# Attention in a two-block language-model kernel: where the next head's Q and K are projected

## What is computed

```python
proj = rmsnorm(x, norm1_g) @ w_in          # dq, dk, dv, fq, fk, fv are slices of it
# diff, for each block of 128 queries:
sc = einsum('bqhcd,bkhcd->bchqk', qb, k) * scale + bias     # causal, -inf above the diagonal
p = softmax(sc);  w = p[:, 0] - lam * p[:, 1];  out = einsum('bhqk,bkhd->bqhd', w, v)
y_diff = rmsnorm(out, diff_subln_g) * (1 - lam_init)
# fox:
sc = einsum('bqhd,bkhd->bhqk', qb, k) * scale + decay       # decay from a running sum, causal
out = einsum('bhqk,bkhd->bqhd', softmax(sc), v)
```

## Time and profile before

| | us |
|---|---|
| median of 3 runs | 3777.13 (3776.09 to 3777.54) |
| the profiled execution | 3780.0 |
| its span (first to last instruction) | 3777.9 |
| TensorE busy in the span | 3231.9 (86%) |
| the two attention stages, from the first V matmul of one to the last `YL` of the other | 87.6 to 717.6 |

### The profile page before, as it was taken

How to read it: one execution, slowest core, us unless ns; L and a number is a source line. 1 busy time by engine, 2 the same in 40 slices (tenths; PEclk the granted TensorE clock), 3 DMA queues, 4 the chain that set the end, 5 groups by cost and what they waited for, 6 DMA issues and landing times. The chain is left out here.

```text
span 3777.9 us, 42591 instructions
## 1 busy us (share of the span) xinstructions
PE 3231.9 (86%) x15247; PEld 2628.9 (70%) x15247; DVE 1374.8 (36%) x2195; ACT 1122.4 (30%) x1533; POOL 771.7 (20%) x510
## 2 busy tenths in 40 slices
PE   5999999899998999899999993586888788996686
PEld 3777777688776777688788872475677676885465
DVE  3244133211155122434434334742224443214743
ACT  3334243212266121412222223122233331332221
POOL 0100100022111121212122110431222221223621
PEclk6999999999999999899999996777899998998878
DMA  2110101022211222311111102403110000211102
GB/s 105 28 34 17 45 23 42 18 67 58 64 38 37 67 68 84 68 39 58 42 47 53 33 28 67 64 0 98 37 39 23 22 22 23 50 50 51 56 17 112
DMA packets 270465, 178.76 MB, mean 47 GB/s; under 512 B 65960, under 2 KB 246312, under 8 KB 269872
## 3 DMA queue, kind: packets, MB, share of 16 engines
q1 hardware_dynamic: 270384, 177.69, 16.8%
HBM read 158.43 MB, written 19.23 MB: 47 GB/s over the span
## 5 line engine op out<-in xcount | busy, mean ns | idle before, releaser
L136 POOL TENSOR_TENSOR w_low<-w_raw,w_high 128x1024 fp32r<-128x1024 f32 (+1 forms) x183 | 418.0, 2284 | 2009.3 <-ACT w_high L129 2004.4
L154 PE MATMUL pu<-act_high,w_high 128*128 128x512 f32 x1104 | 432.8, 392 | 9.5 <-POOLq L108 8.3
L154 PE MATMUL pu<-act_low,w_high 128*128 128x512 f32 x1104 | 431.9, 391 | 0.0
L154 PE MATMUL pu<-act_high,w_low 128*128 128x512 f32 x1104 | 431.7, 391 | 0.0
L129 ACT ACTIVATE w_high<-w_raw 128x1024 fp32r<-128x1024 f32 (+1 forms) x183 | 182.7, 999 | 442.8 <-PE po L950 94.3
L154 PE MATMUL pg<-act_high,w_high 128*128 128x512 f32 x576 | 228.0, 396 | 55.6 <-POOL w_low L136 29.6
L154 PEld LDWEIGHTS pu<-act_high,w_high 128*128 128x128 f32 x1104 | 208.9, 189 | 54.4 <-POOLq L108 9.1
L154 PEld LDWEIGHTS pu<-act_high,w_low 128*128 128x128 f32 x1104 | 208.7, 189 | 43.5
L154 PEld LDWEIGHTS pu<-act_low,w_high 128*128 128x128 f32 x1104 | 208.8, 189 | 43.3
L154 PE MATMUL pg<-act_low,w_high 128*128 128x512 f32 x576 | 226.8, 394 | 0.0
L154 PE MATMUL pg<-act_high,w_low 128*128 128x512 f32 x576 | 226.5, 393 | 0.0
(11 more groups left out here) (508 smaller groups left out, 6788.8 us busy)
## 6 DMA issues: line engine op xcount, KB each, us to landing
w_raw<-in_w_in SPq DMA_DIRECT2D x110, 512.0 KB, 4.2
w_raw<-in_ffn_up SPq DMA_DIRECT2D x44, 512.0 KB, 3.9
w_raw<-in_w_out SPq DMA_DIRECT2D x24, 512.0 KB, 3.9
v_raw<-in_ffn_down SPq DMA_DIRECT2D x11, 1024.0 KB, 5.1
acum_rows<-acum_rows SPq DMA_DIRECT2D x16, 512.0 KB, 3.8
x<-in_x SPq DMA_DIRECT2D x8, 512.0 KB, 8.5
bias<-neg_c SPq DMA_DIRECT2D x4, 1024.0 KB, 5.1
m_part<-gate SPq DMA_DIRECT2D x8, 512.0 KB, 3.1
```

The source lines that it names most:

```text
L136: pool.tensor_tensor(self.low[slot][:, 0:nk, :], self.raw[slot][:, 0:nk, :], self.high[slot][:, 0:nk, :].bitcast(F32), ALU.subtract).then_ ...
L154: last = pe.matmul(out[:, h, :] if not halves else out[h], w[slot][:, k, :], x[:, k, cols], start=(n == 0), stop=(n == 3 * nk - 1))
```

## The change

Q and K each get two buffers, so that the next head's can be written while this head's are read. One of the three transpose banks becomes `pP`, into which the next head's Q and K are projected, half by half (24 matmuls a half, four halves). The 96 matmuls are laid out by a table in 17 places of the head: 6 ahead of the first transposes, 4 to 6 ahead of each `values` and each `turned`, and 9 behind the last `values`. The copies out of `pP` stand at four places of ScalarE's list, the last behind its last transposed group. The loops are over pairs of heads, SyncE's is written out, and the weights of head h + 2 are asked for during head h. The first head's Q and K are projected ahead of the loop.

```diff
+NEXT_HEAD = (("first", 6), (("values", 0), 5), (("turned", 1), 5), (("values", 1), 4), (("turned", 2), 4),
...
+             (("values", 6), 5), (("turned", 7), 5), (("values", 7), 5), ("out", 9))
...
-        Q = sbuf(core, ctx, "q", [P, SEQ])
-        K = sbuf(core, ctx, "k", [P, SEQ])
+        Q = [sbuf(core, ctx, f"q{s}", [P, SEQ]) for s in range(2)]
+        K = [sbuf(core, ctx, f"k{s}", [P, SEQ]) for s in range(2)]
...
-        pT = [psum(core, ctx, f"pt{c}", [P, 4, P]) for c in range(3)]
+        pT = [psum(core, ctx, f"pt{c}", [P, 4, P]) for c in range(2)]
         pO = psum(core, ctx, "po", [P, 4, P])
+        pP = psum(core, ctx, "pp", [P, HALF])
...
-                def head(h, more):
-                    pe.wait_ge(sem("reduced"), h * U + 1)
-                    project(1, h + 2, pS[1])
+                def head(h, s, more):
+
+                    def ahead_of(t, count):
+
+                        for t in range(t, t + count):
+                            g, n = t // (3 * KD), t % (3 * KD)
+                            slot, half = g // 2, g % 2
+                            k, i = n // 3, n % 3
+                            if n == 0:
+                                if half == 0:
+                                    W.wait(pe, slot, h + 3)
+                                if g:
+                                    pe.wait_ge(sem("qk"), h * 4 + 4 + g)
...
-                            pe.wait_ge(sem("ev_act"), h * acts[GN] + acts[max(n - 2, 0)] + 1)
-                            pe.wait_ge(sem("ev_dve"), h * dves[GN] + dves[max(n - 2, 0)] + 1)
+                            pe.wait_ge(sem("ev_act"), h * acts[GN] + acts[max(n - 1, 0)] + 1)
+                            pe.wait_ge(sem("ev_dve"), h * dves[GN] + dves[max(n - 1, 0)] + 1)
...
                     scores(0)
                     scores(1)
+                    project_next("first")
                     turned(0)
                     for i in range(NB):
                         if i + 2 < NB:
                             scores(i + 2)
+                        project_next(("values", i))
                         values(i)
                         if i + 1 < NB:
+                            project_next(("turned", i + 1))
                             turned(i + 1)
-                    if more:
-                        pe.wait_ge(sem("reduced"), h * U + U + 1)
-                        project(0, h + 3, pS[0])
+                    project_next("out")
                     pe.wait_ge(sem("o_scaled"), h + 1)
...
+                        if more and i in TAKEN:
+                            take_next(TAKEN.index(i))
                         if i + 1 < NB:
                             evacuate(h, i + 1)
...
+                    if more:
+                        take_next(3)
 
                     if diff:
                         act.wait_ge(sem("mean"), h + 1)
```

More of the change, by code:

```diff
@@ L846, in _, with next_head_places @@
                 dve.tensor_tensor_scan(c[:, :], f[:, :], z[:, :], 0.0, ALU.mult, ALU.add).then_inc(sem("c"), 1)
+NEXT_HEAD = (("first", 6), (("values", 0), 5), (("turned", 1), 5), (("values", 1), 4), (("turned", 2), 4),
+             (("values", 2), 6), (("turned", 3), 6), (("values", 3), 6), (("turned", 4), 6),
+             (("values", 4), 6), (("turned", 5), 6), (("values", 5), 6), (("turned", 6), 6),
+             (("values", 6), 5), (("turned", 7), 5), (("values", 7), 5), ("out", 9))
+def next_head_places():
+    at, places, taken = 0, {}, []
+    for place, count in NEXT_HEAD:
+        places[place] = (at, count)
+        at += count
+        if at % (3 * KD) == 0 and place != "out":
+            taken.append(place[1] - 1)
+    assert at == 4 * 3 * KD and len(taken) == 3
+    return places, taken
 def stage_attention(core, kind, q_at, k_at, v_at, y0, ahead):
@@ L864, in stage_attention @@
     ends = {(i, c): n + 1 for n, (i, c, _, _) in enumerate(groups)}
+    PLACES, TAKEN = next_head_places()
     with stage(core) as (ctx, sem):
@@ L964, in project, with project_next @@
                                 n += 1
-                        last.then_inc(sem(f"half{slot}") if half == 0 else W.s("used", slot), 1)
-                def head(h, more):
-                    pe.wait_ge(sem("reduced"), h * U + 1)
-                    project(1, h + 2, pS[1])
+                        last.then_inc(sem("half") if half == 0 else W.s("used", slot), 1)
+                def head(h, s, more):
[9 more added lines that the diff above has]
+                                    pe.wait_ge(sem("qk"), h * 4 + 4 + g)
+                            w, x = ((W.high, AH), (W.high, AL), (W.low, AH))[i]
+                            last = pe.matmul(pP[:, :], w[slot][:, k, :], x[:, k, half * HALF:(half + 1) * HALF],
+                                             start=(n == 0), stop=(n == 3 * KD - 1))
+                            if n == 3 * KD - 1:
+                                last.then_inc(sem("half") if half == 0 else W.s("used", slot), 1)
+                    def project_next(place):
+                        if more:
+                            ahead_of(*PLACES[place])
                     def scores(i):
@@ L981, in scores @@
                                 rows = slice(64 * c, 64 * (c + 1))
-                                last[c] = pe.matmul(pS[c][:, a // HALF, 0:e - a], Q[rows, b * P:(b + 1) * P], K[rows, a:e],
+                                last[c] = pe.matmul(pS[c][:, a // HALF, 0:e - a], Q[s][rows, b * P:(b + 1) * P], K[s][rows, a:e],
                                                     start=True, stop=diff or e < n)
@@ L1041, in _ @@
                     pe.wait_ge(sem("mask16"), 2)
-                over_loop(pe, NH, head)
+                over_loop(pe, NH // 2, lambda pair, more: [head(pair * 2 + s, s, more or s == 0) for s in range(2)])
             @block.scalar
@@ L1101, in evacuate @@
                             act.wait_ge(sem("o"), h * U + 2 * (i - 1) + c + 1)
-                        act.activation(PT[:, c, g * P:(g + count) * P], flat(pT[n % 3])[:, 0:count * P], ACT.Copy).then_inc(sem("ev_act"), 1)
+                        act.activation(PT[:, c, g * P:(g + count) * P], flat(pT[n % 2])[:, 0:count * P], ACT.Copy).then_inc(sem("ev_act"), 1)
                 if diff:
                     act.wait_ge(sem("gain_scaled"), 1)
-                over_loop(act, NH, head)
+                over_loop(act, NH // 2, lambda pair, more: [head(pair * 2 + s, s, more or s == 0, more) for s in range(2)])
             @block.vector
```

77 lines of the change are left out of this document (50 added, 27 removed).

## The result

The changed kernel takes **3789.21 us** (median of nine runs, 3783.72 to 3794.78) where the kernel before takes 3777.54 (nine runs beside them): a ratio of 1.0025, with a 95% interval of 1.0015 to 1.0036. That is slower by about 12 us by the medians and 9 by the ratio (6 to 14 by its interval). The sign was forecast, and the time lies in the range of 3782 to 3812, but the size was forecast at +22, about twice as much. The profiled execution takes 3789.49 us with a span of 3787.6, against 3780.0 and 3777.9.

A forecast was written before the change was run, and what follows sets the result against it. TensorE was taken to bound the kernel, except for 4.8 us a head and the lower clock. Three diff heads (15.0), three fox heads (4.2) and two last heads (2.8) sum to +22 us: 3799 us, range 3782 to 3812.

The forecast's parts named there:

- The diff boundary: Between diff heads: 3.8 us idle ahead of the output transposes, 1.6 more ahead of second scores, together +5.4 us.
- The fox boundary: Between fox heads: the bias table's landing makes TensorE wait 2.6 us for second scores instead of 0.74, +1.9 us.
- The fill: Projections put into TensorE's gaps inside the blocks win 2.4 us a diff head, 2.2 a fox head.
- The banks: Two transpose banks make long blocks' transposes wait: net +1.3 us a diff head, +1.0 fox, 1.4 a last head.
- the clock: The low-clock dip moves from the blocks to the boundary and costs about the same 1.5 us a head.
- changes of matmul kind: At the 17 places switching from projection to other matmuls: 0.7 us a head, bounds 0 and 1.5.
- Rival (a): Boundary gaps don't lower the clock: 1.5 us back in six heads, 9 in all, 3790 us; chance 0.17.
- The rest of the program: No term for time outside the two attention stages; counted at nothing.

The follow-up runs named there:

- fox-only run: The change in the fox stage only, the diff stage running the code of the kernel before: 3775.94 us, 0.9988 against the kernel before.
- root first: The changed kernel with ScalarE's table load and square root ahead of the copy of K's second half in diff: 3776.76 us, 0.9995 against the kernel before.
- useless matmuls at the diff boundary: The changed kernel with 14 unread matmuls behind the last values of the three diff heads with a successor: 3789.19 us, 1.0027 against the kernel before.
- the last version: Changed kernel, table load and root before K's copy, 14 projections behind values, `YL` between reductions, bias asked early, projections between first scores and inside transposes: 3742.78 us.
- the early bias: The changed kernel with the bias table asked for right behind the head's last reduction: 3791.82 us, measured in one execution only.

## Why the prediction was right or wrong

**What held.** The diff boundary, in every step up to the output transposes: the copy of K ahead of the table load, the load uncovered, TensorE idle for 3.80 us (forecast 3.8). The table load takes 1.28 and the root starts 0.01 behind it (220.63, then 221.92), so the drain of 1.38 us that the Trainium skill ("ScalarE: Activation LUTs", What ACT_TABLE_LOAD costs) adds does not show ahead of the root; the prediction had counted none. The fox boundary: the bias landing sets the reduction (5.13 us from its issue to VectorE's start, forecast 5.2), TensorE waits 2.43 (forecast 2.6). The fill: the third scores' wait down to 0.77 (forecast 0.7), the waits for values gone. The banks: 0.30 to 0.62 in the four long blocks, forecast 0.45 to 0.76.

**How much the clock took.** The trace tells in which stretches TensorE was granted the lower of its two levels, 1.2 instead of 2.4 GHz. Work there takes twice as long (eight output transposes 1.97 us instead of 1.03), so half of TensorE's busy time in these stretches is an estimate of what the clock cost. One of them, in the first fox head of the kernel before (windows view, columns as above):

```profile
478.90:485.60 6.70, 6.36 (x30) 4.93 (x28) 2.78 (x11) 3.20 (x9) 0.00 (x0) 0.50 0.00 0
```

For the two fox heads of the fox-only run that do the same work, the estimate gives 1.46 us, and their busy times differ by 1.41. From the first V matmul of a stage to the next stage's (in fox to the last output transposes), in us:

| | length | TensorE idle | clock | other busy time |
|---|---|---|---|---|
| diff, before | 315.2 | 26.8 | 10.0 | 278.4 |
| diff, after | 330.3 | 36.9 | 14.2 | 279.2 |
| difference | +15.1 | +10.1 | +4.2 | +0.8 |
| forecast | +16.4 | +14.3 | 0 | +2.1 |
| fox, before | 312.0 | 21.7 | 11.9 | 278.5 |
| fox, after | 308.0 | 23.4 | 3.7 | 281.0 |
| difference | -4.0 | +1.7 | -8.2 | +2.5 |
| forecast | +5.6 | +3.5 | 0 | +2.1 |

(The forecast's idle column is its fill, banks and boundary terms with the last head, its other busy time the 0.7 a head for changes of matmul kind.)

**The step that failed: the clock.** "I expect the dip to move from the blocks to the boundary and to cost about the same 1.5 us." In fox it did not move: the three heads with a successor lost the dip in their blocks, no boundary of the profiled execution got one, and 8.2 us came back that the sum had at nothing. That is most of the 9.6 by which the fox stage missed. It is more than 1.5 a head, since in the kernel before the dips of the first and the last fox head lasted twice as long as the one that the prediction had priced from the earlier trace rows. The prediction argued from the earlier trace rows, a diff row with 3.13 us idle and output transposes behind it, for both stages; the fox boundary has no wait for `o_scaled`, and no row showed what its single gap of 2.6 us does to the clock.

In diff the dip did move to the boundary, and cost more: at the second boundary 0.94 in the output transposes (1.97 - 1.03), 0.31 in the first scores and 1.80 in the second ones (3.79 - 1.99). By the last diff head the low clock lasted through the boundary and into the blocks (0.85 for the whole window). That the diff stage all the same came out near its forecast, +15.1 for 16.4, is luck: the clock took 4.2 us that were not in the sum, the waits came out 4.2 below it and the other busy time 1.3 (the second scores waited 1.49, 1.43 and 1.43 where 2.35 was forecast, in part because the slow work ahead of them filled the time).

Rival (a), that the fill keeps the clock up, split by stage. It had 9 us back, half of them in diff; 8.2 came back in the fox stage and none in diff, so that its time, 3790, fits the result is in part luck too.

That filling the gap ahead of the third scores takes the dip from the blocks was shown from both sides: useless matmuls there made the kernel before 16 us faster, and taking the six projections out of it cost 17, some 13 of them by the estimate above as work at the half clock and most of the rest as waiting.

**Smaller misses.** A fox head adds up as boundary +1.7, fill -2.3, bank waits +0.85 (1.85 in four, against 1.0), clock -1.6, other busy time +0.65, together -0.7, and measures -0.9. So the 0.7 a head for changes of matmul kind was about right in fox; in the middle diff heads the other busy time rose by 0.2 to 0.3 only. The rest of the program, put at nothing, became 1.4 us shorter: 1.9 longer ahead of the stages; behind them 3.3 shorter, 1.3 of it in the first wait of the stage that follows (7.09 us before, 5.78 after) and some 0.8 in its first matmuls, of which fewer ran at half rate. That isn't the change's work: with the six useless matmuls, in a kernel that is otherwise the one before, that wait is 5.69 too, and outside the two stages the twelve profiled executions lie between 3143.0 and 3151.1 us. All together: 16.4 + 5.6 = 22.0 forecast, 15.1 - 4.0 - 1.4 = 9.7 measured in the profiled executions.

**What stays open.** What decides whether a fox boundary lowers the clock. Four profiled executions ran the changed fox stage as it is: the change, root first, fox only, and useless matmuls at the diff boundary. Of their twelve boundaries, with 2.04 to 2.54 us of idle time ahead of the second scores, eight ran on at the full rate and four did not (one in the fox-only run, all three in the last), and the lengths of the gaps do not tell them apart: 2.53 did not lower it, 2.04 did. So the 8.2 us are what this execution got back; by the same estimate the other three got 7.0, 4.5 and 3.7. A forecast of this kernel to better than some 1.5 us for each such head cannot be made from the gaps alone.

**Judging the change.** The move of projections was worth it: the last version is the same idea. What made it slower was what it left at the boundary (3.8 us through one copy in the wrong place of ScalarE's list, `YL` ahead of the first reduction, and nothing between the first scores) and the bank that it took away. Root first alone brings it level with the kernel before, and covering the rest wins 1%.

## What to carry to other kernels

Work that covers a chain of small steps is part of what the chain costs: before it is moved elsewhere, walk the chain on every engine and see what stands in front of each step once the cover is gone, a table load behind a waiting copy above all. A gap on TensorE is priced at its own length and at the half-rate work behind it, and the second must be asked anew at each place, with the gaps of that place; filling 1.4 us of a 2 us gap with useless matmuls won 2 us a head here, since the work behind it no longer ran at half rate. A clock term read from one trace may not come again in the next: the same code with the same gaps had the dip at some boundaries and not at others. A buffer taken away (one transpose bank) can cost as much as the change it makes room for, until other work is put into its waits.

## What the runs showed of the hardware

Six thrown-away matmuls a head made the kernel 16 us faster, mostly by the granted clock: 1.00 instead of 0.97 in the second diff head. And which gap lowers the clock does not go by its length alone: gaps of 2.08 and 0.82 us close together did in the earlier trace rows, 1.93 behind 0.63 did at two of three diff boundaries with useless matmuls, 1.57 did at one of three fox boundaries (the early bias), and a single one of 2.43 did not in the changed kernel and did in the fox-only run.
